# Ten layer norms of a one-core kernel: where TensorE issues the matmuls on the partial sums

## What is computed

```python
def layer_norm(x, g, b):
    mu = jnp.mean(x, axis=-1, keepdims=True)
    xc = x - mu
    var = jnp.mean(xc * xc, axis=-1, keepdims=True)
    return xc * lax.rsqrt(var + LN_EPS) * g + b

def swiglu(x, w_in, w_out):
    gate, up = jnp.split(x @ w_in, 2, axis=-1)
    return (jax.nn.silu(gate) * up) @ w_out

x = layer_norm(ALPHA * x + 0.5 * swiglu(x, w_in, w_out), g, b)
```

## Time and profile before

| what | value |
|---|---|
| time, median of 3 runs | 1805.95 us (1804.25 to 1807.08) |
| the profiled execution's own time | 1804.63 us |
| its span from first to last instruction | 1802.8 us |
| mean granted TensorE clock | 0.988 |
| PE busy | 1764.2 us, 98% of the span |
| DVE busy | 1290.2 us, 72% |
| ACT busy | 977.2 us, 54% |

### The profile page before, as it was taken

How to read it: one execution, slowest core, us unless ns; L and a number is a source line. 1 busy time by engine, 2 the same in 40 slices (tenths; PEclk the granted TensorE clock), 3 DMA queues, 4 the chain that set the end, 5 groups by cost and what they waited for, 6 DMA issues and landing times.

```text
span 1802.8 us, 33249 instructions
## 1 busy us (share of the span) xinstructions
PE 1764.2 (98%) x11768; PEld 1600.3 (89%) x11768; DVE 1290.2 (72%) x2099; ACT 977.2 (54%) x1708; POOL 0.2 (0%) x4
## 2 busy tenths in 40 slices
PE   9999999999999999999999998999999999999998
PEld 7888998888899888888788887889999998898887
DVE  6777789777665776778787766868655568787765
ACT  5564695656355554455465544565534355565543
POOL 0000000000000000000000000000000000000000
PEclk9999999999999999999999999999999999999999
DMA  7665465456545566422356663334455533346562
GB/s 223 189 200 192 127 198 170 149 187 206 180 142 176 189 194 201 138 89 100 104 202 187 196 196 111 117 112 135 140 175 193 181 118 118 112 134 198 186 204 88
DMA packets 76637, 290.77 MB, mean 161 GB/s; under 512 B 9344, under 2 KB 11648, under 8 KB 76544
## 3 DMA queue, kind: packets, MB, share of 16 engines
q1 hardware_dynamic: 76544, 289.50, 50.5%
HBM read 288.42 MB, written 1.05 MB: 161 GB/s over the span
## 4 chain that ended last, share of the span: by engine, by line
PE 91%; DVE 5%; ACT 2%; issue 1%; DMA 0%; SPq 0%; ACTq 0%; DVEq 0%
PE psum L500 33%; PE psum L501 17%; PE psum L492 11%; PE psum L494 11%; PE psum L493 11%; DVE wlo L1508 1%; PE psum L632 1%; PE psum L738 1%; PE psum L627 1%; DVE r L1680 1%; PE psum L579 1%; PE psum L737 1%; ACT whi L1043 1%; PE psum L860 1%; PE psum L867 1%
## 5 line engine op out<-in xcount | busy, mean ns | idle before, releaser
L1508 DVE TENSOR_TENSOR wlo<-raw,whi 128x1024 fp32r<-128x1024 f32 (+3 forms) x496 | 644.8, 1309 | 245.9 <-ACT whi L1043 245.1
L500 PE MATMUL psum<-x_split,whi 128*128 128x512 f32 x1760 | 618.4, 395 | 3.6 <-DVE x_split L1543 2.1
L1043 ACT ACTIVATE whi<-raw 128x1024 fp32r<-128x1024 f32 (+3 forms) x496 | 548.7, 1119 | 40.4 <-PE psum L494 21.5
L501 PE MATMUL psum<-x_split,wlo 128*128 128x256 f32 x1760 | 494.6, 281 | 0.0
L500 PEld LDWEIGHTS psum<-x_split,whi 128*128 128x128 f32 x1760 | 331.3, 188 | 81.8 <-DVE x_split L1543 2.5
L492 PE MATMUL psum<-x_split,whi 128*128 128x272 f32 (+1 forms) x1184 | 346.3, 293 | 4.6 <-DVE x_split L1716 3.4
L494 PE MATMUL psum<-x_split,wlo 128*128 128x272 f32 (+1 forms) x1184 | 338.6, 286 | 0.0
L493 PE MATMUL psum<-x_split,whi 128*128 128x272 f32 (+1 forms) x1184 | 337.7, 285 | 0.0
L501 PEld LDWEIGHTS psum<-x_split,wlo 128*128 128x128 f32 x1760 | 332.2, 189 | 0.0
L500 PE MATMUL psum<-h_split,whi 128*128 128x512 f32 x770 | 272.2, 397 | 0.0
L492 PEld LDWEIGHTS psum<-x_split,whi 128*128 128x128 f32 x1184 | 223.4, 189 | 14.9 <-issue 9.1
(11 more groups left out here) (231 smaller groups left out, 1769.8 us busy)
## 6 DMA issues: line engine op xcount, KB each, us to landing
raw<-w_in SPq DMA_DIRECT2D x264, 512.0 KB, 3.5
raw<-w_out SPq DMA_DIRECT2D x96, 704.0 KB, 4.4
raw<-w_mix SPq DMA_DIRECT2D x44, 512.0 KB, 3.6
raw<-w_rg SPq DMA_DIRECT2D x25, 512.0 KB, 4.1
raw<-w_q SPq DMA_DIRECT2D x24, 512.0 KB, 3.7
raw<-w_mixo SPq DMA_DIRECT2D x16, 576.0 KB, 3.7
raw<-w_kv SPq DMA_DIRECT2D x16, 512.0 KB, 3.7
raw<-w_rg_out SPq DMA_DIRECT2D x8, 640.0 KB, 3.9
```

The costliest lines, as they stand in the source:

```text
L500: nc.tensor.matmul(ps[:, bank, :], whi[slot][:, w], split, start=start, stop=False)
L501: return nc.tensor.matmul(part(bank, 0), wlo[slot][:, w], split[:, 0], start=False, stop=stop)
L1043: nc.scalar.activation(whi[slot][:, 0:cols], raw[slot][:, 0:cols], ACT.Copy).then_inc(w_hi_done, count)
L1508: V.tensor_tensor(wlo[slot][:, 0:cols], raw[slot][:, 0:cols], f(whi[slot][:, 0:cols]), ALU.subtract).then_inc(w_lo_done, 1)
```

## The change

The first of the three groups of matmuls (the wait on `sums_done`, `means` and `token_means` on `sums`) leaves `layer_norm` and is issued inside the last chunk of the output stage, in front of its last four row tiles (`SUMS_BEHIND`), by a new function `sums_inside` that `from_h` and `half` call ahead of every row tile. It acts only in the last chunk and at that one row tile. `means` and `token_means` become functions of the whole block, with the column count as an argument and the flags for first and last given by the caller. All ten norms behind a stage are changed; "emb" keeps its order.

```diff
+SUMS_BEHIND = 4
...
+        def means(T, tile, first=False, last=False):
+            return nc.tensor.matmul(acc(4, T), ones_d, tile[:, tok0(T):TOK], start=first, stop=last)
+
+        def token_means(T, tile, col, first=False, last=False):
+
+            starts = token_starts(T)
+            for m, c in enumerate(starts):
+                ins = nc.tensor.matmul(ps[:, 5, col + m:col + m + 1], tile[:, c:c + P], ones_d[:, 0:1], start=first and m == 0,
+                                       stop=last and m == len(starts) - 1, skip_group_check=True)
+            return ins
+
+        def sums_inside(st, i, j, left):
+
+
+            if isinstance(i, int) and SLOTS * i + j == st.chunks - 1 and left == SUMS_BEHIND:
+                T = tokens[st.name]
+                pe.wait_ge(sums_done, norm_stages.index(st.name) + 1)
+                means(T, sums[:, 0, :], first=True)
+                token_means(T, sums[:, 0, :], 0, first=True)
+                token_means(T, sums[:, 1, :], 4)
+
         def from_h(st, i, j, tiles, ready=None, begun=None):
...
+                sums_inside(st, i, j, len(todo) - n)
                 last = h_products(st, i, j, k, len(todo) == tiles and n == 0, n == len(todo) - 1)
...
+                    sums_inside(so, i, j, HALF_F - t)
                     if two_parts(so) and not (isinstance(i, int) and 4 * i + j >= so.chunks - 2):
...
             else:
-                pe.wait_ge(sums_done, norm_stages.index(name) + 1)
-                means(sums[:, 0, :], first=True)
-                token_means(sums[:, 0, :], 0)
-                token_means(sums[:, 1, :], 4)
-
                 pe.wait_ge(acc_free, by_name[name].u0 + by_name[name].units)
-                means(r[:, KD - 1, :], last=True).then_inc(mean_done, 1)
-                token_means(r[:, KD - 1, :], 0)
+                means(T, r[:, KD - 1, :], last=True).then_inc(mean_done, 1)
+                token_means(T, r[:, KD - 1, :], 0)
                 pe.wait_ge(sq_done, KD * (n + 1))
-                ins = token_means(sq[:, KD - 1, :], 4, True)
+                ins = token_means(T, sq[:, KD - 1, :], 4, last=True)
```

More of the change, by code:

```diff
@@ L621, in layer_norm @@
             T = norms[n][1]
-            t = slice(tok0(T), TOK)
             starts = token_starts(T)
[L624 to L635, removed]
             if name == "emb":
@@ L641, in layer_norm @@
                     pe.wait_ge(y_done, k + 1)
-                    ins = means(r[:, k, :], k == 0, k == KD - 1)
+                    ins = means(T, r[:, k, :], k == 0, k == KD - 1)
                 ins.then_inc(mean_done, 1)
                 pe.wait_ge(emb_squares, 1)
-                ins = token_means(sums[:, 1, :], 4, True)
+                ins = token_means(T, sums[:, 1, :], 4, first=True, last=True)
             else:
-                pe.wait_ge(sums_done, norm_stages.index(name) + 1)
-                means(sums[:, 0, :], first=True)
-                token_means(sums[:, 0, :], 0)
-                token_means(sums[:, 1, :], 4)
                 pe.wait_ge(acc_free, by_name[name].u0 + by_name[name].units)
-                means(r[:, KD - 1, :], last=True).then_inc(mean_done, 1)
-                token_means(r[:, KD - 1, :], 0)
+                means(T, r[:, KD - 1, :], last=True).then_inc(mean_done, 1)
+                token_means(T, r[:, KD - 1, :], 0)
                 pe.wait_ge(sq_done, KD * (n + 1))
-                ins = token_means(sq[:, KD - 1, :], 4, True)
+                ins = token_means(T, sq[:, KD - 1, :], 4, last=True)
             ins.then_inc(stat_done, 1)
```

## The result

The changed kernel takes 1825.25 us (median of 5 runs, 1823.56 to 1827.7) against 1805.95 before: 19.3 us more, a ratio of 1.011 (95% interval 1.0096 to 1.0124). The forecast was 1820.7, 14.8 us more, with a range from 1815 to 1826. The profiled execution is the longest of the five, 1827.7, with a span of 1825.9.

A forecast was written before the change was run, and what follows sets the result against it. PE's program order bounds the kernel (PE 91% of the span); 4.0 for out0 to out5, 8.4 for rg_out, o, mixo0 and mixo1, and 2.4 for the clock make 14.8 us over 1805.95: 1820.7 us, range 1815 to 1826.

The forecast's parts named there:

- the clock falls in all four late norms: Rival: in rg_out, o, mixo0, mixo1 block and 12 matmuls run at the lower clock; 17 to 22 us, chance 0.14.
- the main case: All ten norms slower, with half the matmuls behind the wait at lower clock in half of four norms; 14.8 us, chance 0.50.
- early group, lost cover of the eviction: Norms of out0 to out5: sums in time, but the block no longer hides DVE's last eviction; 0.67 each, 4.0 us.
- late group, 12 matmuls and a bare eviction behind the sums' arrival: Norms of rg_out, o, mixo0, mixo1: PE stops for the sums, r starts 2.08 (mixo0 2.16) later; 8.4 us.
- lower clock behind the stops: In rg_out, o, mixo0, mixo1: half the block and 12 matmuls at 1.2 GHz in half the norms; 2.4 us.
- The rival of passing matmuls: In rg_out, o, mixo0, mixo1 the 12 ready matmuls pass the waiting block; 6.7 us in all, 1812.7, chance 0.07.
- The rival of the free block: Inside the chunk the block's weight loads fit beside full matmuls, adding no time; -1.5 us, 1804.5, chance 0.05.
- 3.55 us from the sums to r: In o: block 1.47, 12 matmuls 1.29, then 0.79 to the last tile's matmul, where it had been 1.47 in all.
- the sentence that the fall is covered by the norm's vector work: In the norms before the change, the clock falls while PE waits for vector work, so the fall costs nothing.

The follow-up runs named there:

- early group alone: Changed kernel with the block on the sums inside the chunk only in out0 to out5, the other four norms as before: 1809.46 us, ratio 1.0031 against before.
- filled stop: Changed kernel plus 11, 20, 13 and 14 filling matmuls ahead of the wait on the sums in rg_out, o, mixo0, mixo1: 1819.2 us, ratio 1.0082 against before.
- the opposite direction: Kernel before, first sums awaited alone behind the chunk; in rg_out, o, mixo0, mixo1 DVE evicts before last squares and weight work, second-sums matmuls later: 1802.58 us, ratio 0.9987.
- the stop alone: Kernel before plus a wait for the sums ahead of the last four row tiles in rg_out, o, mixo0, mixo1, block still behind the chunk: 1813.01 us, ratio 1.005.
- late group alone: Changed kernel with the block on the sums inside the chunk only in rg_out, o, mixo0, mixo1, out0 to out5 as before: 1821.44 us, ratio 1.0092 against before.

## Why the prediction was right, and which term was too small

**Direction and mechanism.** Right on each step that moves work, and too low on the clock. The time lies inside the range by 0.75 us; two of the five runs (1826.09 and 1827.7) lie above it. What the trace shows is the rival "the clock falls in all four late norms", given a chance of 0.14 and 17 to 22 us, and not the main case, in which half of them lose it. That the stated range held is in part luck: it took in the lower half of that rival. The forecast of 14.8 us was made of three terms:

| term | predicted | measured |
|---|---|---|
| early group, lost cover of the eviction | 4.0 | 5.1 (early group alone); 5 x 0.78 + 0.77 = 4.7 from the trace |
| late group, 12 matmuls and a bare eviction behind the sums' arrival | 8.4 | 8.5 from the filled stop: r 3.53, 3.52 and 3.53 us behind the block's start against 1.46, 1.47 and 1.47, mixo0 4.11 against 1.82 |
| lower clock behind the stops | 2.4 (bounds 0 and 9.6) | 4.5 to 6.0 (changed kernel less filled stop) |
| sum | 14.8 | 19.3 |

**The early group.** The sums were in time, no stop appears, and r starts 0.80 us behind the chunk's last matmul (0.79 predicted). The predicted 0.67 is 0.78, mostly because the first fp32r matmul behind the block is 0.08 us slower; the prediction took the chunk to be longer by the block alone. DVE's wait before the first centring is 0.79 us, where 0.8 was named.

**The late group.** PE stopped 1.24 us in rg_out, 2.70 in o, 1.58 in mixo0 and 1.60 in mixo1 (1.4 to 2.4 predicted), and no row tile ran in the meantime. The rival of passing matmuls falls: in o 12 ready matmuls stood behind the wait for 2.70 us. The rule of the Trainium skill that matmuls keep program order ("TensorE: Matmul & The Clock Gate", packing small matmuls) agrees with this. The rival of the free block falls as well: inside the chunk of out0 it takes 195.80 - 194.56 = 1.24 us, as behind it. The block of about 0.6 us that the prediction worked out for this rival would not have made it hold either, as by its own limit a gain needs less than 0.57.

That 3.55 us from the sums to r came out at 3.52 is in part luck. The 1.47 us that the prediction took for the block is the distance to r, which in o hung on the eviction (913.90); behind a stop the block itself takes 1.34 us (917.63 to 918.97 in the filled kernel). The 12 matmuls behind it take 1.39, not 1.29. The two errors cancel.

**The clock** is the term that was mis-sized. The prediction let half of the block and the 12 matmuls run at the lower level in half of the four norms, and nothing behind r. The trace has the lower level in all four late norms, and it lasts into the norm: r starts 4.30 to 5.74 us behind the sums (3.5 to 4 predicted), and from r to the spread it is 4.0 us in rg_out, o and mixo1 instead of about 2.5, which no other work covers. In the profiled execution, the longest of the five, the late norms lose 14.1 us from the sums' arrival to r (8.4 of it by program order) and 5.1 from r to the 200th matmul of the next stage, so 10.8 of clock, over the upper bound of 9.6; the median of the runs says 4.5 to 6.0. The step that failed is the sentence that the fall is covered by the norm's vector work: this holds where the clock falls late in the norm, as in o before (1.6 us behind r, and the 200th product matmul comes 41.35 us behind r, against 41.34 in rg_out, whose clock stayed up), and not where it falls in front of r, when the mean, the one-column matmuls and the spread run at half pace too. The trace of before already held a case against that sentence. In mixo0 the clock fell 1.1 us behind r:

```profile
1255.84 0.70 PE L627 MATMUL psum<-r,con 128*128 128x272 f32 x2
...
1256.90:1260.20 3.30, 3.30 (x17) 3.30 (x18) 1.51 (x5) 1.42 (x3) 0.00 (x0) 0.50 0.34 135
```

There the 200th product matmul comes 33.31 us behind r, and 32.12 in the filled kernel, whose clock stayed up: 1.2 us that nothing covered.

**What stays open.** Between the kernel with the filled stop (14.8) and its two terms (5.1 and 8.5) 1.2 us are left. Its profiled execution has low-clock stretches elsewhere than the one of before: it loses 1.3 us in stage rg, where 0.50 lasts 10.2 us and not 6.8, and 1.3 us behind out4, and is 1.0 us ahead in other places. For the medians, with runs of before that reach from 1802.9 to 1805.8 beside it, this was not taken apart. Why the clock falls behind one stop and not behind another was not settled either.

## What to carry to other kernels

Work that already lies beside another engine's wait is free only there: moved forward into a stretch that the engine fills anyway, it adds its full length there and leaves the wait bare (together 0.78 us a norm here). A wait drawn forward in an in-order queue holds everything that was ready behind it, so read first when its semaphore is raised against the place where the wait will stand, in each stage for itself: six of ten norms had the sums in time, and the four others made most of the loss. Where such a wait binds, look at the engine that is late: the opposite direction, with DVE's order changed too, was the only kernel here that gained (1.9 us).

## What the runs showed of the hardware

58 added matmuls, whose results nobody reads, took 4.5 to 6.0 us off the time of the changed kernel; with them the granted clock stayed at 1.00 behind the four stops in the profiled execution.

An idle time alone did not set the clock: 2.55 us of idle time in o with full matmuls behind it left it at 1.00 in the profiled execution of the kernel with the stop alone, while 2.70 us with the block behind it were followed by 0.50 in the changed kernel. The block behind it did not decide either. In mixo1 PE stops equally long in the changed kernel and in the one with the late group alone, with the same block behind the stop; first the line of the changed kernel:

```profile
1614.18 0.87 PE L548 MATMUL psum<-sums,con 128*128 128x256 f32 x2 [1.60 <-DVE sums L1639]
```

and that of the late group alone:

```profile
1612.26 0.70 PE L549 MATMUL psum<-sums,con 128*128 128x256 f32 x2 [1.60 <-DVE sums L1645]
```

In the changed kernel the clock fell 0.4 us behind the start of the block, and r came 5.66 us behind that start; in the other it fell only 2.8 us behind r, and r came after 3.53.

What a fall cost depended on where in the norm it came. In front of r or at it, as behind the four stops and in o of the kernel with the early group alone, the 200th product matmul came 1.4 us later behind r (42.7 instead of 41.34 us with 256 columns). Behind the spread, as in mixo1 before the change, it cost nothing (41.34).
